# Residues of the weights on VectorE alone, written over the raw pieces, in a float32 network on one core

## The reference

```
def _swiglu(h, w1, w3, w2):            # silu(h @ w1) * (h @ w3) @ w2
x = first_block(x, norm_mix, w_in, ..., ffn_w1, ffn_w3, ffn_w2, router, moe_w1, moe_w3, moe_w2)
return second_block(x, even_norm_w_2, even_w_in_2, ..., odd_w_in_2, ..., odd_w_out_2)
```

## Time and profile before

| what | value |
|---|---|
| median of 3 runs | 2482.8 us (2481.63 to 2483.01) |
| the profiled execution | 2489.43 us, its span 2487.6 us |
| PE, DVE, ACT, POOL busy | 2254.0, 1247.0, 886.4, 506.2 us |
| mean granted TensorE clock | 0.915 of full speed |
| weights loaded | 320 MB, the 16 DMA engines busy 42% by the main queue |

### The profile page before, as it was taken

The page is one execution under the profiler, slowest core; times in us unless marked ns, Lnnn a source line. Parts: engine busy times, 40 slices in busy tenths (PEclk is TensorE's granted clock), DMA queues, the critical chain, the costliest instruction groups (busy, mean ns, idle before and its releaser), DMA issues.

```text
span 2487.6 us, 40335 instructions
## 1 busy us (share of the span) xinstructions
PE 2254.0 (91%) x17862; PEld 2155.2 (87%) x17862; DVE 1247.0 (50%) x1820; ACT 886.4 (36%) x994; POOL 506.2 (20%) x176
## 2 busy tenths in 40 slices
PE   6788988998887998999999999999888988998897
PEld 6778988998777898999999999999888876888776
DVE  3863654665774364444444444444483455432553
ACT  3333343333433233344343433433344321233242
POOL 1200122221200111222222222222212122012210
PEclk9889998998988999899999999999899987578877
DMA  5221353554321235255555554555678652033310
GB/s 207 85 69 60 109 188 119 187 179 148 119 69 40 81 127 192 95 194 178 185 191 170 192 185 160 190 180 177 146 124 153 97 93 84 1 100 104 102 52 18
DMA packets 270575, 320.15 MB, mean 129 GB/s; under 512 B 5440, under 2 KB 252992, under 8 KB 270272
## 3 DMA queue, kind: packets, MB, share of 16 engines
q1 hardware_dynamic: 269648, 316.18, 42.2%
q10 hardware_dynamic: 752, 1.38, 0.1%
HBM read 316.49 MB, written 1.05 MB: 128 GB/s over the span
## 4 chain that ended last, share of the span: by engine, by line
PE 79%; DVE 12%; ACT 4%; issue 2%; DMA 1%; POOL 1%; SPq 0%; DVEq 0%; POOLq 0%; ACTq 0%
PE b L336 77%; DVE s_arena L347 4%; DVE s_wl L426 2%; ACT s_wh L356 1%; PE b L1782 1%; DVE s_arena L350 1%; DMA s_ring<-even_w_in 1%; DVE s_roots L347 1%; POOL s_wl L426 1%; DVE s_roots L369 0%; DMA s_ring<-w_in 0%; ACT s_arena L359 0%; DVE s_roots L350 0%; DVE s_arena L1737 0%; DVE s_arena L1734 0%
## 5 line engine op out<-in xcount | busy, mean ns | idle before, releaser
L336 PE MATMUL b<-s_Hh,s_wh 128*128 128x256 f32 x3240 | 943.8, 291 | 39.4 <-issue 20.7
L336 PE MATMUL b<-s_Hl,s_wh 128*128 128x256 f32 x3240 | 928.5, 287 | 0.0
L336 PE MATMUL b<-s_Hh,s_wl 128*128 128x256 f32 x3240 | 927.8, 286 | 0.0
L426 DVE TENSOR_TENSOR s_wl<-s_ring,s_wh 128x2048 fp32r<-128x2048 f32 (+1 forms) x219 | 478.8, 2187 | 653.5 <-ACT s_wh L356 653.3
L426 POOL TENSOR_TENSOR s_wl<-s_ring,s_wh 128x2048 fp32r<-128x2048 f32 (+2 forms) x109 | 458.3, 4205 | 1600.6 <-ACT s_wh L356 1600.6
L356 ACT ACTIVATE s_wh<-s_ring 128x2048 fp32r<-128x2048 f32 (+1 forms) x328 | 574.0, 1750 | 508.9 <-PE b L336 495.1
L336 PEld LDWEIGHTS b<-s_Hh,s_wh 128*128 128x128 f32 x3240 | 634.6, 196 | 51.4 <-issue 36.2
L336 PEld LDWEIGHTS b<-s_Hl,s_wh 128*128 128x128 f32 x3240 | 634.4, 196 | 0.4
L336 PEld LDWEIGHTS b<-s_Hh,s_wl 128*128 128x128 f32 x3240 | 633.5, 196 | 0.0
L336 PE MATMUL b<-s_arena_r,s_wh 128*128 128x256 f32 x2592 | 482.2, 287 | 28.3 <-DVE s_arena_r L347 13.5
L336 PEld LDWEIGHTS b<-s_arena_r,s_wh 128*128 128x128 f32 x2592 | 412.0, 195 | 32.5 <-DVE s_arena_r L347 14.0
(11 more groups left out here) (149 smaller groups left out, 1553.4 us busy)
## 6 DMA issues: line engine op xcount, KB each, us to landing
s_ring<-moe_w SPq DMA_DIRECT2D x120, 1024.0 KB, 5.1
s_ring<-ffn_w SPq DMA_DIRECT2D x33, 1024.0 KB, 4.9
s_ring<-w_gate SPq DMA_DIRECT2D x32, 1024.0 KB, 5.0
s_ring<-even_w_in SPq DMA_DIRECT2D x32, 1024.0 KB, 9.8
s_ring<-w_in SPq DMA_DIRECT2D x26, 1024.0 KB, 5.0
s_ring<-odd_w_in SPq DMA_DIRECT2D x16, 1024.0 KB, 5.1
s_ring<-moe_w SPq DMA_DIRECT2D x24, 512.0 KB, 3.5
s_ring<-w_out SPq DMA_DIRECT2D x8, 1024.0 KB, 5.0
```

The costliest lines, as they stand in the source:

```text
L336: return e.matmul(out, l, r, start=start, stop=True, skip_group_check=True)
L426: e.tensor_tensor(lo, raw_of(i), hi.bitcast(F), SUB).then_inc(*up(lo_engine(i), "lo", i))
```

## The change

`RAW` becomes 6. The tile `wl` is gone; its memory goes to three more slots of `ring`, so that the use of on-chip memory stays as it was. `ring_lo` is the same memory as `ring`, typed fp32r, and the residue of a piece is written there over its own raw values. All residues are in VectorE's list: `lo_engine` is gone, and each `rests` forms every piece that comes due. The load of piece i waits for "used" of piece i-6 instead of the residue of piece i-3. GpSimd keeps its clears, one mask, the norms' residues (L506) and the cosine products; the generators that only placed its weight residues are gone, and `conf_pool`, `rwkv_pool` and `turn_pool` run as plain functions.

```
-RAW = 3
+RAW = 6
-        X_, ring_ = sb("X", 2048), sb("ring", RAW * SLOT)
+        X_ = sb("X", 2048)
+        ring_at = nc.sbuf_base
+        ring_ = sb("ring", RAW * SLOT)
+        ring_lo = nc.alloc_sbuf_tensor_at("s_ring_lo", [128, RAW * SLOT], R, offset=ring_at)
...
         def parts_of(i):
-            q = i % PARTS
+            q, s = i % PARTS, i % RAW
             n = LOADS[i].kt * LOADS[i].n
-            return wh_[:, q * SLOT:q * SLOT + n], wl_[:, q * SLOT:q * SLOT + n]
+            return wh_[:, q * SLOT:q * SLOT + n], ring_lo[:, s * SLOT:s * SLOT + n]
...
-        def lo_engine(i):
-            return "G" if i % 3 == 1 else "V"
...
         def rest_piece(e, i):
             hi, lo = parts_of(i)
-            if lo_engine(i) == "G":
-                pool_free(e)
             e.wait_ge(*on("hi", i))
-            e.tensor_tensor(lo, raw_of(i), hi.bitcast(F), SUB).then_inc(*up(lo_engine(i), "lo", i))
+            e.tensor_tensor(lo, raw_of(i), hi.bitcast(F), SUB).then_inc(*up("V", "lo", i))
...
-        def rests(e, engine, i):
+        def rests(e, i):
             for j in range(0 if i == 0 else i + AHEAD, min(i + AHEAD + 1, len(LOADS))):
-                if lo_engine(j) == engine:
-                    rest_piece(e, j)
+                rest_piece(e, j)
...
-            walk(PLAN, bulk=bulk_pool(e, l), K=rwkv_pool(e, l), C=conf_pool(e, l))
-            for j in range(4):
-                rests(e, "G", li[f"wo{l}", j])
+            conf_pool(e, l)
+            rwkv_pool(e, l)
...
                 if i >= RAW:
-                    e.wait_ge(*on("lo", i - RAW))
+                    e.wait_ge(*on("used", i - RAW))
```

More of the change, by code:

```diff
@@ L262, in build @@
         P_ = sb("par", pn)
-        X_, ring_ = sb("X", 2048), sb("ring", RAW * SLOT)
+        X_ = sb("X", 2048)
+        ring_at = nc.sbuf_base
+        ring_ = sb("ring", RAW * SLOT)
+        ring_lo = nc.alloc_sbuf_tensor_at("s_ring_lo", [128, RAW * SLOT], R, offset=ring_at)
         h_at = nc.sbuf_base
-        Hh_, Hl_, wh_, wl_ = (sb(k, n, dt=R) for k, n in (("Hh", 2048), ("Hl", 2048), ("wh", PARTS * SLOT), ("wl", PARTS * SLOT)))
+        Hh_, Hl_, wh_ = (sb(k, n, dt=R) for k, n in (("Hh", 2048), ("Hl", 2048), ("wh", PARTS * SLOT)))
         R_ = sb("roots", 336)
@@ L707, in bulk_dve @@
             rest_branch(3)
-            rests(e, "V", li[f"b3{l}", 0])
+            rests(e, li[f"b3{l}", 0])
             for f in range(4):
@@ L715, in bulk_dve @@
             for j in range(4):
-                rests(e, "V", li[f"rt{l}", j])
+                rests(e, li[f"rt{l}", j])
                 yield
@@ L723, in bulk_dve @@
                 p = li[f"g{i}{l}", f]
-                rests(e, "V", p)
+                rests(e, p)
                 yield
-                rests(e, "V", p + 1)
+                rests(e, p + 1)
                 e.wait_ge(*on("ev", l, 23 + 2 * n))
@@ L735, in bulk_dve @@
                     stt(e, lo, Mo, 0.5, hi.bitcast(F), MUL, SUB).then_inc(*up("V", "MP lo", l, f))
[L736 to L747, removed]
                 yield
@@ L1015, in conf_pool @@
             e.memset(c_up[:, :, 0:30], 0.0).then_inc(*up("G", "conv pad", l))
-            for _ in range(26):
-                yield
         def rwkv_pe(e, l):
@@ L1319, in rwkv_pool @@
             e.memset(kz, 0.0).then_inc(*up("G", "zeroed", l))
-            for _ in range(8):
-                yield
             msk = c("lvl")[:, 0:64].unsqueeze(1).broadcast_to([128, 8, 64])
@@ L1325, in rwkv_pool @@
             e.tensor_tensor(Am, m3(Gm)[:, :, 0:64], msk, MUL).then_inc(*up("G", "level mask", l, 0))
-            for _ in range(28):
-                yield
         PLAN = (". .K .K .K" + " .KC" * 4 + " .KSC" * 9 + " .KS" * 5 + " .KC" * 13 + " .K" * 4 + " ." * 13).replace(" ", "")
@@ L1390, in mix_dve @@
                 e.wait_ge(par_in, 16)
-                rests(e, "V", 0)
+                rests(e, 0)
             norm_dve(e, n, M)
@@ L1489, in up_dve @@
             v = tmp[s % 2][:, 0:m, :]
-            rests(e, "V", p)
-            rests(e, "V", p2)
+            rests(e, p)
+            rests(e, p2)
             e.wait_ge(*on("half tanh", name, j))
@@ L1553, in ffn_pool @@
             norm_pool(e, 1, f_tmp)
[L1554 to L1559, removed]
         MOE_RING = [B[2], B[3], B[0]]
@@ L1666, in moe_pool @@
             norm_pool(e, 3, m_tmp)
[L1667 to L1674, removed]
         def qk_evac(e, i, u, b, raw, sq, f0):
@@ L1979, in dil_dve @@
                     silu_dve(e, p, b, e_gt, e_g[:, 2 * j:2 * j + 2, :])
[L1980 to L1987, removed]
                     yield
@@ L2247, in even_pool @@
             norm_pool(e, 4, zs)
-            for name, j in CONV:
-                rests(e, "G", li[name, j])
             e.wait_ge(c2_in, 16)
-            walk(EVEN, bulk=dil_pool(e), Q=turn_pool(e, "even", e_tiles, e_tmps))
-            for j in range(6):
-                rests(e, "G", li["eo.2", j])
+            turn_pool(e, "even", e_tiles, e_tmps)
         oa = Arena(0)
@@ L2341, in oddp_dve @@
                 yield
[L2343 to L2349, removed]
         def odd_pe(e):
@@ L2392, in odd_pool @@
             norm_pool(e, 5, o_raw)
-            walk(ODD, bulk=oddp_pool(e), Q=turn_pool(e, "odd", o_tiles, o_tmps))
-            for j in range(4):
-                rests(e, "G", li["oo.2", j])
+            turn_pool(e, "odd", o_tiles, o_tmps)
         def tensor_program(e):
```

19 lines of the change are left out of this document (5 added, 14 removed).

## The result

The changed kernel takes 2455.4 us in the median (2451.6 to 2456.6, 4 runs) against 2482.5: ratio 0.9892, interval 0.9879 to 0.9904, so 27.1 us less. The forecast was 24 less, 2459, in the range 2438 to 2480. The profiled executions were 2489.4 before and 2456.6 after, 33 us apart, mostly since that one execution of before was 7 above its median; the first experiment is about this.

The account below looks back on a forecast made before the run. TensorE, busy 91% of the span, was taken to bound the kernel. Terms of -5.5, -10.0, -2.4, -3.0, -2.0, -0.2 and about -1 gave -24 us: 2482.8 to 2458.8, with 2438 to 2480 to hold 8 in 10.

Parts of the forecast that it names:

- product at 72: Layer 0's start: a 0.69 us product took 4.11; a residue now precedes it but begins some 1.8 us earlier: -1.5 us.
- first level's mask (taps at 150): Layer 0: 4.24 us of VectorE stall beside a GpSimd residue go, a 2.29 us residue comes: -1.9 us.
- the trap: Layer 0, near 207: a residue waiting for ScalarE now stands ahead of the level mask, TensorE waiting for it: +3.0 us.
- convolutions: Even layer: a 4.1 us stall goes and a 2.29 us residue comes, -1.8; a half-size piece gives -0.6; together -2.4 us.
- late loads: Even layer: the load issued at 1873.00 can go 6.2 us earlier; between 0 and -5.6 us, taken as -3.0.
- odd layer: At 2322 a stall goes, -1.5 us; at 2370 and 2394 residues ahead of path work, +1.3; sum -0.2 us.
- FFN: TensorE is nearly full there, so the moved residues were counted as 0.
- small sites: Remaining small places, not itemised, taken together as about -1 us.
- rival 1: VectorE's order costs more than the lock: residues queued ahead of path work, 3.0 us each; 2495 with 12 more; chance 0.12.
- rival 3: More than the sum: shorter waits return TensorE clock, another 10 to 21 us, say 2443 us; chance 0.14.
- Rival 4: Early loads share the queue, making the start 6 us later: -18, 2465 us, inside the forecast's range; no separate chance.
- Rival 2: Stalls were spare time, TensorE waiting for something else there; a third of the sum remains, -8: 2475 us; chance 0.12.

Follow-up runs that it names:

- the first experiment: The kernel before, unchanged, profiled a second time: one execution of 2477.0 us.
- e1: The kernel before with every residue on VectorE and nothing else, three raw slots kept: 2457.1 us, ratio 0.9899.
- e5: The changed kernel with five slots, GpSimd also subtracting constants into an unread spare tile at every third piece: 2503.9 us; five slots alone, 2456.0.
- e6: The changed kernel with five slots, GpSimd also clearing an unread spare tile five times at every third piece: 2459.8 us; five slots alone, 2456.0.
- step-first kernel: The changed kernel with RWKV's step ahead of the bulk's residue in every group of VectorE's list in the two mixers: 2426.9 us, ratio 0.9779.

## Why the prediction was right

The mechanism is shown, not only argued: e1 has it without the ring, e5 brings the stalls back with work that no residue depends on, e6 shows that for VectorE's two-source instructions the reading does it. The steps, by TensorE's idle time, before and after:

| step | forecast | measured |
|---|---|---|
| start | -2.0 | 10.75 to 8.74: -2.0 |
| product at 72 | -1.5 | all waits from there to 110: -0.4, and -1.4 against the second profile of before |
| first level's mask (taps at 150) | -1.9 | 8.24 to 6.20: -2.0 |
| fourth level's mask, the trap | +3.0 | 1.63 to 4.64: +3.0 idle, and +2.6 of clock |
| residue at 346 | -1.6 | 1.55 to none: -1.6 |
| product at 360 | -1.5 | 7.20 to 5.67: -1.5 |
| taps at 673, layer 1 | -3.2 | 6.68 to 0.93, then 3.09 to 5.80: -3.0 |
| mask at 817 | -2.5 | 2.54 to none: -2.5 |
| root at 897 | -4.3 | 4.40 to 0.10: -4.3 |
| convolutions | -2.4 | waits for residues 9.5 to 7.8: -1.7 |
| late loads | -3.0 | 5.56 to 3.55: -2.0 |
| queries and keys | -2.0 | 2 x 0.97 to none: -1.9 |
| odd layer | -0.2 | 0.72 to 1.80, 3.11 to 1.53, none to 0.65, 1.39 to 2.86, 0.54 to none: +1.1 |
| FFN | 0 | 1.79 to 0.81: -1.0 |
| experts | 0 | 693.1 us before and after: 0.0 |
| small sites | about -1 | -3.7, the rest of the 23.5; the largest 8.40 to 7.46 behind the even layer's state-space steps |

What made the large terms hold is the cap: a stall counted only as far as TensorE stood idle for it. The total is closer than its terms, and that is luck. The product at 72, the convolutions, the late loads and the odd layer gave 4.1 us less than forecast, by the first profile of before; the FFN, where the stall at L1505 was on the path once, and the small sites gave 3.7 more. In the odd layer the +1.1 hangs on the place that went from 0.72 to 1.80: it is 0.80 in the kernel with one mask moved, whose odd layer is the same code.

Two more things were off, both in size. The trap was read as one place. It was rival 1's mechanism, and it was there at every level of the solve; that it did not cost more is because most of those residues stood there before. It made the change lose 5.6 us in one place, not 3.0. And the clock was left out of the sum and stood as rival 3. Its share of the change is not shown. Of the 27.1 us 23.5 are waits, and the other 3.6 busy time by subtraction only: the interval goes from 23.8 to 30.0 us, and against the two profiles of before TensorE's busy time is 9.3 less or 3.1 more. That shorter waits do give clock back is shown by the step-first kernel, 12.1 us.

The Trainium skill's paragraph on offloading (Perfetto Trace Analysis, "Optimizing Scalar/DVE Operations"), weighed for the convolutions, has two halves. The first, that help may make sense where VectorE is saturated, did not hold there; its warning of the shared port did. VectorE was busy 86%, two residues came onto it, and the stretch that goes from 1805 to 1859 in the trace of before got shorter, from 54.1 to 51.5 us.

Rival 4 is excluded: with six loads let go at once, TensorE's first waits are no longer (22.86 against 24.79 us for its first norm products), and the kernel with all residues on VectorE and three slots has the same waits there to 0.1 us. Rival 2 is too, since 23.5 of 24 came. Two slips of the prediction change nothing: the middle of 0 and -5.6 is -2.8 and not -3.0, and the chances for "faster" add up to 0.87 and not 0.86.

## What to carry to other kernels

Before work is shared between VectorE and GpSimd, look in the trace for VectorE instructions that are several times their usual length and end with a GpSimd instruction: here 458 us of "free" help on an idle engine cost more than doing the work on VectorE. Count such a stall only up to TensorE's idle time behind it: nine of the places then came out within 0.2 us here, while the other terms were off by some 4 us either way and cancelled. And when filler work stands in an in-order list, put it behind the step that the path waits for: moving whole residues by one place in the list gained as much as the change itself, nearly half of it in TensorE's clock. In the convolutions, where TensorE wanted the residue itself, the same move lost 2.5 us.

## What the runs showed of the hardware

Two executions of the same kernel differ by 12.4 us in TensorE's busy time with idle times equal to 0.1 us. A wait of 4.6 us cost 2.6 us more at a lower clock behind it in layer 0 and 0.9 in layer 1, one of 1.6 us none, in the same place. GpSimd's clears leave VectorE's products of 128 x 512 at 0.693 us and stretch a `TENSOR_SCALAR` by up to the 0.95 us of one clear; its 109 reading instructions add 110 us to VectorE's busy time. At the fourth level's mask, in the reading kernel, a mask of 0.68 us took 3.94:

```profile
214.40 3.94 DVE L1285 TENSOR_TENSOR s_arena<-s_arena,s_c 128x512 f32<-128x512 f32 x1
```
